# Layer 2's convolution norm: squares in two buffers, its root refined in two steps, and all steps set denser along the attention blocks

## The reference, cut to what matters

```python
u = a * jax.nn.sigmoid(gate)                          # 512 channels
u = causal_depthwise_conv(u, conv_w, conv_b)          # width 31
u = jax.nn.silu(layer_norm_2(u, conv_ln_g, conv_ln_b))
u = rms_norm(u, conv_out_g)
# beside it: q, k, v of 8 heads, softmax over visible chunks, rms_norm(o, attn_out_g)
def layer_norm_2(x, g, b):
    mu = jnp.mean(xf, axis=-1, keepdims=True)
    var = jnp.mean(jnp.square(xf - mu), axis=-1, keepdims=True)
    y = (xf - mu) * lax.rsqrt(var + EPS)
    return (y * g + b).astype(x.dtype)
```

## Time and profile before

| | us |
|---|---|
| median of 3 runs | 3557.8 (3557.28 to 3564.66) |
| the profiled execution | 3553.04 |
| its span | 3550.9 |
| TensorE busy, DVE busy, ACT busy | 3397.2, 1778.6, 1119.2 |
| blocks 0 to 159, from the first rotation of queries to the first output product | about 1467 to 1789 of the span |
| the stretch of the convolution's norms | about 1656 to 1764 |

### The profile page before, as it was taken

One profiled execution on the slowest core, in us unless ns is written; L12 is line 12 of the kernel. 1 busy time (PEld: TensorE's weight loads), 2 busy tenths in 40 slices (PEclk: granted clock), 3 DMA queues, 4 the chain that ended last, 5 costly groups with the idle time before them and its releaser, 6 DMA issues.

```text
span 3550.9 us, 39250 instructions
## 1 busy us (share of the span) xinstructions
PE 3397.2 (96%) x16240; PEld 2781.4 (78%) x16240; DVE 1778.6 (50%) x1897; ACT 1119.2 (32%) x1493; POOL 1087.9 (31%) x1144
## 2 busy tenths in 40 slices
PE   8998999999999999898799999999999999999997
PEld 6665768888888688555499999999987788888776
DVE  4666563222223578777547546446474423444532
ACT  4443352111112532444533111111142533333442
POOL 3111344222333333100014334334334222222253
PEclk9999999999999999899899999999999999999998
DMA  3000311111111221000021111111113111011242
GB/s 126 24 26 28 107 66 64 49 48 48 48 48 49 71 90 36 24 7 7 6 78 42 48 48 48 48 48 44 48 41 110 51 66 54 30 36 35 78 142 95
DMA packets 56249, 192.21 MB, mean 54 GB/s; under 512 B 6900, under 2 KB 7284, under 8 KB 55560
## 3 DMA queue, kind: packets, MB, share of 16 engines
q1 hardware_dynamic: 56072, 189.71, 15.4%
HBM read 172.83 MB, written 16.86 MB: 53 GB/s over the span
## 4 chain that ended last, share of the span: by engine, by line
PE 81%; DVE 13%; ACT 4%; issue 1%; DMA 0%; POOL 0%; DVEq 0%; ACTq 0%; SPq 0%; POOLq 0%
PE psum L270 21%; PE psum L271 21%; PE psum L272 21%; PE psum L138 11%; DVE mix L107 3%; DVE work L98 2%; PE psum L324 2%; PE psum L325 2%; PE psum L326 2%; DVE res L98 1%; DVE softmax_shift_columns L113 1%; PE psum L136 1%; DVE u_padded L98 1%; ACT L126 1%; DVE res L107 1%
## 5 line engine op out<-in xcount | busy, mean ns | idle before, releaser
L98 POOL TENSOR_TENSOR w_lo<-w_raw,w_hi 128x256 fp32r<-128x256 f32 x1140 | 1087.7, 986 | 2428.2 <-ACT w_hi L131 2428.2
L270 PE MATMUL psum<-x_hi,w_hi 128*128 128x512 f32 (+2 forms) x3240 | 1200.7, 371 | 12.6 <-DVE mix L98 5.9
L271 PE MATMUL psum<-x_lo,w_hi 128*128 128x512 f32 (+2 forms) x3240 | 1165.0, 360 | 0.0
L272 PE MATMUL psum<-x_hi,w_lo 128*128 128x512 f32 (+2 forms) x3240 | 1161.4, 358 | 0.0
L131 ACT CAST w_hi<-w_raw 128x1024 fp32r<-128x1024 f32 x285 | 298.3, 1048 | 1509.9 <-PE psum L272 1436.9
L270 PEld LDWEIGHTS psum<-x_hi,w_hi 128*128 128x128 f32 x3240 | 612.7, 189 | 104.1 <-issue 20.7
L271 PEld LDWEIGHTS psum<-x_lo,w_hi 128*128 128x128 f32 x3240 | 612.3, 189 | 82.1 <-issue 17.5
L272 PEld LDWEIGHTS psum<-x_hi,w_lo 128*128 128x128 f32 x3240 | 610.6, 188 | 70.2
L270 PE MATMUL psum<-h_hi,w_hi 128*128 128x512 f32 x824 | 325.2, 395 | 3.1 <-DVE res L98 3.1
L272 PE MATMUL psum<-h_hi,w_lo 128*128 128x512 f32 x824 | 320.8, 389 | 0.0
L271 PE MATMUL psum<-h_lo,w_hi 128*128 128x512 f32 x824 | 320.7, 389 | 0.0
(11 more groups left out here) (281 smaller groups left out, 3727.2 us busy)
## 6 DMA issues: line engine op xcount, KB each, us to landing
w_raw<-w_dram SPq DMA_DIRECT2D x285, 512.0 KB, 3.2
res<-spill SPq DMA_DIRECT2D x4, 1044.0 KB, 9.6
res<-x_dram SPq DMA_DIRECT2D x8, 512.0 KB, 8.9
res<-x_dram SPq DMA_DIRECT2D x4, 1024.0 KB, 8.0
spill<-res SPq DMA_DIRECT2D x1, 4096.0 KB, 13.9
spill_a<-mix SPq DMA_DIRECT2D x8, 512.0 KB, 2.7
res<-spill_a SPq DMA_DIRECT2D x8, 512.0 KB, 4.6
x_plain<-spill SPq DMA_DIRECT2D x4, 1024.0 KB, 10.7
```

Source lines behind the costliest of these rows:

```text
L98: self.mark(self.e.tensor_tensor(out, a, b, op), inc)
L270: t.e.matmul(out, whi, xhi, start=k == 0, stop=False, skip_group_check=True)
L271: t.e.matmul(out, whi, xlo, start=False, stop=False, skip_group_check=True)
L272: ins = t.e.matmul(out, wlo, xhi, start=False, stop=last_k, skip_group_check=True)
```

## The change

The branch gets 95 steps instead of 91 in the first 140 blocks, so that steps come at shorter distances. Squares of rows 1 and 3 go to `A[2]`, that of row 2 to `A[3]`; a square waits only for the use of its own buffer. DVE adds each square one step after ACT has made it. The refinement is split in two steps of two instructions. Idle steps are put in so that the three generators agree.

```diff
-    STEPS, LAST_STEP = 91, 140
+    STEPS, LAST_STEP = 95, 140
...
-            for _ in range((5, 12, 0)[n]):
+            for _ in range((6, 14, 0)[n]):
                 yield True
...
-        for c, (ready, freed) in enumerate(((2, 0), (3, 0), (5, 4), (7, 6))):
+        for c, (ready, freed) in enumerate(((2, 0), (3, 0), (4, 0), (6, 5))):
             a.wait_ge(self.u_step_v, max(ready, freed))
-            a.act(A[2] if c else A[0], M[c], ACT.Square, inc=self.u_step_a)
+            a.act((A[0], A[2], A[3], A[2])[c], M[c], ACT.Square, inc=self.u_step_a)
             yield True
         for n in range(2):
+            yield True
             yield True
             self.act_sums(a, 1 + n, A[3], 1.0)
...
-            for _ in range(4):
+            for _ in range(5):
                 yield True
...
-                a.wait_ge(self.u_step_v, (10, 10, 11, 12)[c])
-                a.act(A[2] if c else A[0], M[c], ACT.Square, inc=self.u_step_a)
+                a.wait_ge(self.u_step_v, (10, 10, 10, 11)[c])
+                a.act((A[0], A[2], A[3], A[2])[c], M[c], ACT.Square, inc=self.u_step_a)
                 yield True
...
-        for c in range(4):
-            v.tt(M[c], M[c], A[1], ALU.subtract, inc=self.u_step_v)
-            if c:
-                v.wait_ge(self.u_step_a, c + 1)
-                v.tt(A[0], A[0], A[2], ALU.add, inc=self.u_step_v)
+        def add(c, square):
+            v.wait_ge(self.u_step_a, square)
+            v.settle()
+            v.tt(A[0], A[0], A[3 if c == 2 else 2], ALU.add, inc=self.u_step_v)
+
+        for c in range(5):
+            if c < 4:
+                v.tt(M[c], M[c], A[1], ALU.subtract, inc=self.u_step_v)
+            if c > 1:
+                add(c - 1, c)
             yield True
...
-            k.root_newton(v, A[1], A[2], A[3], 4 * P, EPS, inc=self.u_step_v)
+            v.tt(A[2], A[1], A[1], ALU.mult)
+            v.settle()
+            v.stt(A[2], A[3], 4 * P * EPS, A[2], ALU.add, ALU.mult)
+            yield True
+            v.settle()
+            v.ts(A[2], A[2], -0.5 / (4 * P), 1.5, ALU.mult, ALU.add)
+            v.settle()
+            v.tt(A[1], A[1], A[2], ALU.mult, inc=self.u_step_v)
             yield True
...
             yield True
+            yield True
             for c in range(4):
                 if c:
-                    v.wait_ge(self.u_step_a, 10 + c)
-                    v.settle()
-                    v.tt(A[0], A[0], A[2], ALU.add, inc=self.u_step_v)
+                    add(c, 10 + c)
                 yield True
```

## The result

The changed kernel takes 3564.81 us (median of 16 runs, 3560.4 to 3568.2), the kernel before in the same comparison 3556.21 us (16 runs, 3553.1 to 3564.7). The ratio is 1.0025, 95% interval 1.0019 to 1.0032: slower by 8.6 us. Forecast was +3.8 us, 3561.5, in a range of 3549 to 3571.

What follows compares the result with a forecast made beforehand. TensorE, 81% of the chain, was taken to bound the kernel, so only its waits and clock count. Terms −3.0 − 0.2 + 2.9 + 2.4 + 0.7 + 1.0 = +3.8 us on 3557.8 gave 3561.5, range 3549 to 3571.

Steps and rivals of the forecast that it cites:

- the grid in heads 0 to 3: An extra tap in place 8 of heads 0 and 2 lengthens the chain to `dve_head_out`: +0.7 us, bounds 0 and +4.3.
- Adds at place 14 of head 4: Three adds right ahead of `dve_head_out` lengthen the wait before block 98's scores: +2.9 us, and +2.4 for the clock.
- Refinement of head 5: Refinement in places 10 and 11, guess in place 9: blocks 111 to 118 take 18.3 us; −3.0 us.
- Squares: Squares in two buffers, added a step later; place 7 of head 5 loses its 3.17 us wait; squares themselves 0.
- Refinement of head 6: Refinement in places 12 and 14, guess one place earlier: blocks 133 to 138 take 13.5 us; −0.2 us.
- Silu in place 19: Silu starts earlier; waits of 7.0 us instead of 5.7, clock loss of 4.3 kept: +1.0 us, bounds −4.3 and +4.
- The clock stays up: Rival: shorter, scattered waits in heads 5 and 6 keep the clock at full speed; 3550 to 3555 us, chance 0.16.
- The exchange was the whole cost: Rival: early guess puts both refinement halves under matrix work, removing waits and clock loss; −8, 3550 us, chance 0.10.
- Grid only, +3 to +7: Rival: buffers and split leave the order of waits as it was, only the grid acts; +3 to +7 us, chance 0.05.
- the copy behind the Silu: Rival: block 120's wait for ACT's copy passes 5 us, clock falls there and in heads 0, 2; +11.4, 3569 us, chance 0.17.

Runs made afterwards that it cites:

- e1: The changed kernel with DVE's three adds of the rows moved from block 94 to block 95, behind `dve_head_out`: 3565.7 us.
- e2: The changed kernel with one tap of head 4 moved from block 83 (place 3) to block 84 (place 4): 3557.9 us.
- e5: The changed kernel with both halves of each refinement joined again in one step: 3560.9 us.
- e6: The changed kernel with all squares back in one buffer, each added in the step of its own square: 3569.4 us.
- h1: The changed kernel's norm steps, each in the block where its work stands in the kernel before, without the denser grid: 3557.4 us.
- e3: The changed kernel with taps of heads 0 to 4 in their old blocks, adds in block 97, first sum in 98: 3556.0 us.
- g1: The kernel before with only its 63 taps redistributed, at most one in places 9 to 14 of each head: 3542.7 us.

## Why the prediction was right, and where it was not

The direction and the range held. That the sum of 3.8 came within 3.0 us of the stretch's 6.8 is luck: by the table, parts came out slower than forecast by 8.2 us together, and others faster by 5.2. Two terms were mis-sized by about 4 us, the grid in heads 0 to 3 and the Silu, and one place had no term.

*Adds at place 14 of head 4, +2.9 and +2.4.* Right. Forecast was a wait of about 4.0 and a clock near 0.5 behind it; it is 4.05 and 0.51, and the part takes +4.65 for +5.3, half in idle time and half by the clock. What e1 adds: the wait isn't the property of this place.

*The grid in heads 0 to 3, +0.7.* It is +4.6, just over the bound of 4.3, but that bound was made of falls of the clock, and what happened is not. Waits of 1.55 and 1.58 became 2.80, and the clock fell behind both (0.57 over 4.00 us each, 1.7 us). But the fall that before has in head 3, from 1609 to 1617 for 3.1 us, is gone. Up to block 84 the clock costs 9.8 us before and 10.0 after. What grew is TensorE's idle time, from 14.1 to 18.4 us: 2.5 at the two waits, and waits of 0.78 and 1.56 us before the scores of blocks 38 and 78 (heads 1 and 3), where before there is none; ahead of block 78 TensorE then ran at the lower clock. I took the lower end because I let DVE's idle time of 0.91 absorb the tap, and I priced heads 1 and 3 at nothing because their taps keep their places. In heads 0 and 2 a second tap comes ahead of the head's piece, as the rows of DVE above show.

*Head 4, place 3: missed.* +3.1 us, and e2 takes back 2.9 there. I had looked at places 8 to 15 only. The order of blocks 82 and 83 shows two taps ahead of a head's piece, and I priced none.

*Refinement of head 5, −3.0.* The size of the piece was right, its cause wrong. Blocks 111 to 118 take 18.1 us, forecast 18.3. But DVE had a gap of 2.53 us for the guess, and the largest wait is one I did not name: TensorE's product with values at 1709.59 waits 3.20 us for ACT's head copy, which stands behind guess and loads. The split has no part in it (e5: the same 3.20 in the same place). What moved the time was the place of the chain. Ahead of it, blocks 105 to 111 take 3.3 us more, by the second sum, counted with 1.9, and by the clock, down from 1693 to 1697 for 1.7 us, unforeseen. So the part came to −1.7 us.

*Squares, 0, bounds 0 and +1.* Wrong as a statement on the buffers: on this grid they are worth 7.4 us (e6; 4.6 by the medians), on the old one nothing with the split together (h1). I read the 21.6 us of DVE's idle time for ACT as going with the places. In after two groups of that stretch read (1673 to 1783; count, busy, mean ns, idle before, releaser):

```profile
L98 DVE TENSOR_TENSOR u_padded<-u_padded 128x1044 f32<-128x1044 f32 x10 | 13.1, 1310 | 10.7 <-ACT u_padded L126 10.3
L98 DVE TENSOR_TENSOR mix<-mix,u_padded 128x1044 f32<-128x1044 f32 x8 | 9.7, 1243 | 4.7 <-ACT u_padded L126 4.6
```

10.7 us for 21.6, where near 5 was expected. My count left out the guess, for which DVE waits in both kernels: 4.3 us before (2.13 twice) and 4.9 after. For squares alone it is 17.2 us before and 5.4 after. The 4.7 us of the second row are new: DVE comes 4.58 us early for the copy of the first sum.

*Refinement of head 6, −0.2.* 13.15 us for 13.5 forecast and 13.68 before. The split doesn't win there, as said.

*Silu in place 19, +1.0, bounds −4.3 and +4.* The other term mis-sized by about 4 us. The wait is 4.81 (forecast 5.0) and the next 2.06 (forecast 2.0 in pieces). But blocks 118 to 133 take 3.3 us less, since the clock behind the Silu costs 2.9 instead of the 4.3 that I kept, and the fall of 1.8 us behind block 118 is gone with the 4.17 us wait ahead of it. TensorE's idle time grew by 0.8 us, near the forecast; the clock's cost fell by 3.2. I priced no clock for the wait that I had bought off.

*The rivals.* "The clock stays up" fell: the clock costs 5.9 us more. "The exchange was the whole cost", 3550, fell with the direction. "Grid only, +3 to +7" was priced too low: +13.4. That the copy behind the Silu would tip it fell too, as its wait stayed under 5 us. The rule of the Trainium skill (TensorE: Matmul & The Clock Gate, "A second HAM failure mode: psum-queue depth-cycling") fits h1, which has the 4.17 us waits halved and a dearer clock (26.3 us for 20.8). No run tests it alone, and e2 and after, with the same waits and falls of 1.5 and 4.7 us around block 138, show that the waits ahead of a fall don't decide by themselves what it costs.

## What to carry to other kernels

When a step joins an evenly spaced grid, all steps move; price each of them by what it now stands ahead of on its engine. List, for every place, the instruction for which the busiest engine waits next, and look for a second step of 1.3 us ahead of it. A wait taken from one place (e1, e3) comes back at the next consumer of the same late engine unless its work is moved to where that engine has idle time (g1), and a buffer or a split is worth only what the places leave to save: 7.4 us on one grid, nothing on another.

## What the runs showed of the hardware

Moving one tap by one block changed the stretch by 6.3 us where the wait and its clock fall explain 2.9. Another 3.0 came some 50 blocks later, from a fall of the clock that cost 1.5 us instead of 4.7 behind the same waits. So a sum of waits, however well forecast, is in this stretch uncertain by about 3 us.

A tap takes 1.30 us, and more while POOL works on `w_lo`. Timeline of before, DVE's tap in the place discussed above, and POOL at that time:

```profile
1631.50 1.60 DVE L107 SCALAR_TENSOR_TENSOR mix<-u_padded,vectors,mix 128x1044 f32<-128x1044 f32 x1 [0.40 <-ACT work L131]
```
```profile
1631.27 5.89 POOL L98 TENSOR_TENSOR w_lo<-w_raw,w_hi 128x256 fp32r<-128x256 f32 x4 [69.17 <-ACT w_hi L131]
```

The four instructions of POOL take 1.47 us each, for 0.99 in the mean of the whole kernel. Head 2 shows the same, a tap of 1.59 us at 1556.45 beside POOL's four from 1556.21, again of 1.47 us. The Trainium skill (SBUF — State Buffer, "SBUF: two separate sides") calls the port that both engines share an exclusive lock, by which one waits until the other's instruction ends; 0.3 us more is less than one whole instruction of POOL, and these rows don't tell a lock from a slowdown.
